# Low halves of the weights in two GpSimd operations each, and ScalarE's high halves placed ahead of its waits in one projection

## The reference, cut to what matters

```python
def second_block(x, ...):
    h = rmsnorm(x, ln1_g[l])
    proj = h @ w_in[l]
    b_a, c_a, x_a, x_b, g_b, gate_a_logit, gate_b_logit = jnp.split(proj, SPLIT_POINTS, axis=-1)
    y_a = b_a * causal_depthwise_conv(c_a * x_a, conv_a_w[l])
    u_b = causal_depthwise_conv(x_b, conv_b_w[l], conv_b_b[l])
    y_b = rg_lru(u_b, lru_wa[l], lru_ba[l], lru_wx[l], lru_bx[l], lru_lambda[l])
    y_b = y_b * jax.nn.gelu(g_b)
    ...
```

## Time and profile before

| | us |
|---|---|
| median of 3 runs (lowest, highest) | 1902.72 (1899.79, 1903.24) |
| the profiled execution's own time | 1900.95 |
| its span in the trace | 1898.9 |
| TensorE busy | 1763.8 |
| VectorE busy | 971.0 |
| GpSimd busy | 751.6 |
| ScalarE busy | 633.9 |

### The profile page before, as it was taken

One profiled execution on the slowest core, in us unless ns is written; L12 is line 12 of the kernel. 1 busy time (PEld: TensorE's weight loads), 2 busy tenths in 40 slices (PEclk: granted clock), 3 DMA queues, 4 the chain that ended last, 5 costly groups with the idle time before them and its releaser, 6 DMA issues.

```text
span 1898.9 us, 21690 instructions
## 1 busy us (share of the span) xinstructions
PE 1763.8 (93%) x7718; PEld 1424.0 (75%) x7718; DVE 971.0 (51%) x1285; ACT 633.9 (33%) x789; POOL 751.6 (40%) x312
## 2 busy tenths in 40 slices
PE   6899998885799898999999999999999999999996
PEld 4677875663678686888888877777888888888885
DVE  5752387888862447242334676767323343133136
ACT  3322342232242341122114456566333343222222
POOL 3342441113334143444444345455444444444442
PEclk9899998987899998999999999999999999999998
DMA  4232221111222022222222323232222222222222
GB/s 160 89 111 78 89 86 37 34 45 45 89 89 89 23 92 75 100 90 98 99 97 91 103 97 111 99 100 99 90 99 99 96 93 99 97 91 100 100 91 97
DMA packets 47695, 169.28 MB, mean 89 GB/s; under 512 B 5205, under 2 KB 5205, under 8 KB 47321
## 3 DMA queue, kind: packets, MB, share of 16 engines
q1 hardware_dynamic: 44640, 160.45, 24.6%
q10 hardware_dynamic: 3000, 8.09, 1.2%
HBM read 166.43 MB, written 2.10 MB: 89 GB/s over the span
## 4 chain that ended last, share of the span: by engine, by line
PE 29%; issue 29%; POOL 14%; DVE 1%; POOLq 0%; ACT 0%; DVEq 0%
POOL m_w_lo L439 14%; PE ps L471 10%; PE ps L473 10%; PE ps L472 10%; DVE m_h L1948 0%; DVE m_s L1209 0%; POOLq L447 0%; POOLq L445 0%; POOL m_QL L459 0%; DVE m_qs L1581 0%; PE ps L499 0%; DVE m_qs L1583 0%; DVE m_ftmp L1573 0%; DVE m_ftmp L1571 0%; DVE m_s L1923 0%
## 5 line engine op out<-in xcount | busy, mean ns | idle before, releaser
L439 POOL TENSOR_TENSOR m_w_lo<-m_raw,m_w_hi 128x1024 fp32r<-128x1024 f32 x302 | 737.2, 2444 | 1073.0 <-ACT m_w_hi L881 1072.8
L881 ACT ACTIVATE m_w_hi<-m_raw 128x1024 fp32r<-128x1024 f32 x302 | 318.1, 1056 | 652.6 <-DMA m_raw<-in_strips 648.9
L471 PE MATMUL ps<-m_XH,m_w_hi 128*128 128x512 f32 x1160 | 470.7, 406 | 10.6 <-POOL m_w_lo L439 8.8
L472 PE MATMUL ps<-m_XL,m_w_hi 128*128 128x512 f32 x1160 | 455.6, 393 | 0.0
L473 PE MATMUL ps<-m_XH,m_w_lo 128*128 128x512 f32 x1160 | 455.4, 393 | 0.0
L471 PEld LDWEIGHTS ps<-m_XH,m_w_hi 128*128 128x128 f32 x1160 | 220.4, 190 | 75.9 <-POOL m_w_lo L439 17.5
L472 PEld LDWEIGHTS ps<-m_XL,m_w_hi 128*128 128x128 f32 x1160 | 220.6, 190 | 46.6 <-issue 2.4
L473 PEld LDWEIGHTS ps<-m_XH,m_w_lo 128*128 128x128 f32 x1160 | 220.1, 190 | 47.2
L471 PE MATMUL ps<-m_FH,m_w_hi 128*128 128x512 f32 x432 | 169.1, 391 | 2.9 <-DVE m_FL L1202 2.8
L472 PE MATMUL ps<-m_FL,m_w_hi 128*128 128x512 f32 x432 | 168.7, 390 | 0.0
L473 PE MATMUL ps<-m_FH,m_w_lo 128*128 128x512 f32 x432 | 168.6, 390 | 0.0
(11 more groups left out here) (310 smaller groups left out, 2260.1 us busy)
## 6 DMA issues: line engine op xcount, KB each, us to landing
m_raw<-in_strips SPq DMA_DIRECT2D x302, 512.0 KB, 3.2
m_x_in<-in_x ACTq DMA_DIRECT2D x8, 256.0 KB, 4.3
m_x_res<-in_x ACTq DMA_DIRECT2D x1, 2048.0 KB, 8.0
out<-m_h SPq DMA_DIRECT2D x8, 256.0 KB, 2.1
m_memf<-in_mem ACTq DMA_DIRECT2D x1, 1024.0 KB, 10.2
m_decay<-in_decay ACTq DMA_DIRECT2D x1, 1024.0 KB, 14.9
m_w<-in_w ACTq DMA_DIRECT2D x1, 512.0 KB, 13.3
m_skip<-in_skip ACTq DMA_DIRECT2D x1, 512.0 KB, 3.7
```

Source lines behind the costliest of these rows:

```text
L439: nc.gpsimd.tensor_tensor(w_lo[:, c], raw[:, c], f(w_hi[:, c]), ALU.subtract).then_inc(lo_ready, 1)
L471: pe.matmul(dst, w_hi[:, c], xh, start=first, stop=False)
L472: pe.matmul(dst, w_hi[:, c], xl, start=False, stop=False)
L881: act.activation(w_hi[:, c], raw[:, c], ACT.Copy).then_inc(hi_ready, 1)
```

## The change

`low` writes a strip's low half in two operations of 512 columns, each of which counts `lo_ready` up by one, so every wait for it on TensorE is doubled; TensorE still waits for both. In `lru_turn` three of the six `ahead` calls of a turn move up in ScalarE's list: w4's ahead of the wait for `m_pX`, w5's ahead of the wait for the convolution, and w3' into the turn before, between the square and the square root. In the first turn w3's stays where it was; the last turn gives none for the strips after it, which the next loop does.

```diff
@@ GpSimd @@
             def low(slot):
-                c = slice(slot * STRIP, (slot + 1) * STRIP)
-                nc.gpsimd.tensor_tensor(w_lo[:, c], raw[:, c], f(w_hi[:, c]), ALU.subtract).then_inc(lo_ready, 1)
+                for part in range(2):
+                    c = slice(slot * STRIP + part * (STRIP // 2), slot * STRIP + (part + 1) * (STRIP // 2))
+                    nc.gpsimd.tensor_tensor(w_lo[:, c], raw[:, c], f(w_hi[:, c]), ALU.subtract).then_inc(lo_ready, 1)
@@ TensorE, and so at six more waits @@
-                pe.wait_ge(lo_ready, n + 1)
+                pe.wait_ge(lo_ready, (n + 1) * 2)
@@ ScalarE, lru_turn @@
                 n = S_IN + mt * 6
-                ahead(n)
                 if mt == 0:
+                    ahead(n)
                     root(4)
                     root(5, acc)
+                ahead(n + 1)
                 act.wait_ge(in_free[0], mt + 1)
                 act.activation(xtap[:], pX[:, 3:T + 3], ACT.Identity, bias=col("cbb", mt), scale=col("cb3", mt)
                                ).then_inc(x_tap, 1)
-                ahead(n + 1)
+                ahead(n + 2)
                 act.wait_ge(u_full, mt + 1)
                 act.activation(uH[:], t2[1][:], ACT.Copy).then_inc(u_high, 1)
-                ahead(n + 2)
                 act.wait_ge(a_in, mt + 1)
...
                 act.activation(a_sq[:], t2[8][:], ACT.Square).then_inc(lru_e, 1)
+                if mt < KT - 1:
+                    ahead(n + 6)
                 act.wait_ge(lru_q, mt + 1)
```

More of the change, by code:

```diff
@@ L722, in _ @@
             for u in range(4):
-                pe.wait_ge(lo_ready, S_WOUT + u + 1)
+                pe.wait_ge(lo_ready, (S_WOUT + u + 1) * 2)
                 for k in range(4, KT):
@@ L832, in in_turn @@
                     n = v * 6 + 5
-                    pe.wait_ge(lo_ready, i * 12 + (S_IN + n + 1))
+                    pe.wait_ge(lo_ready, (i * 12 + (S_IN + n + 1)) * 2)
                     pe.wait_ge(u_pair, mt + 1)
```

## The result

The changed kernel takes 1873.3 us (median of four runs, 1868.13 to 1876.67) beside 1902.49 for the kernel before, a ratio of 0.9847 [0.9822, 0.9871]. The forecast was 1886 with a range of 1876 to 1898: right in direction, too small by 13 us, and the range missed.

What follows compares the result with a forecast made beforehand. A closed ring of VectorE and ScalarE, stretched by GpSimd's low halves, was taken to bound the input projection. 1900.95 - 14 (projection) - 3 (elsewhere) = 1884, with the median 1.8 us above: 1886 us, range 1876 to 1898.

Steps and rivals of the forecast that it cites:

- Elsewhere: Outside the input projection, only the split acts, mainly in the first 520 us: 3 us gained, bounds 0 to 24.
- The projection: In the input projection's seven turns and the merge's head, split and moves together gain 14 us.
- the ring: VectorE and ScalarE handing work to each other in each projection turn: 31.09 us, falling to 29.15, TensorE alone 28.56.
- four late starts: In each projection turn, strips w3, w4, w0' and w1' start late on TensorE, losing 2.5 us over four.
- Rival 1: GpSimd holds VectorE over both halves, 2.5 us or more; projection turn near 31 us, total 1898 to 1904; chance 0.07.
- Rival 2: A half costs far more than half, from 1.6 us the projection loses; at 1.7 us total 1914; chance 0.04.
- Rival 3: Modest gain: halves of 1.35 to 1.45 us, projection gains 5 to 9, nothing outside; 1893 to 1898; chance 0.16.
- Rival 4: More gained outside the projection, 12 us, with TensorE the limit in the projection; about 1873; chance 0.13.
- 22 low halves: Low halves in early mLSTM, convolution, query and key stretches; each could give back up to about 1.1 us.

Runs made afterwards that it cites:

- e3: Kernel before, with two operations per strip everywhere except the input projection and the first four merge strips: 1887.09 us, 0.9911.
- e5: Kernel before, with two operations only for the 58 strips up to the long convolution's end: 1892.88 us, 0.9951.
- e13: Kernel before, with two operations only for the 12 z projection strips, whose low halves fall in the mLSTM stage: 1901.62 us, 0.9990.
- e8: Changed kernel, with two operations per strip only in the input projection and first four merge strips, whole elsewhere: 1886.53 us, 0.9914.
- e4: Changed kernel, with w3's high half moved behind the gelu, no longer ahead of the square root's table load: 1868.13 us, 0.9806.
- e11: The changed kernel itself, unaltered, measured again: 1868.05 us, 0.9824 of the kernel before.
- e2: Kernel before with only the moves in ScalarE's list, low halves whole: 1901.43 us, 0.9987.
- e1: Kernel before with only the split into two operations, ScalarE's list as before: 1868.52 us, 0.9806.
- e14: Kernel before, with each strip's low half in sixteen operations of 64 columns, ScalarE's list as before: 1917.28 us, 1.0073.
- e7: Kernel before, with each strip's low half in four operations of 256 columns, ScalarE's list as before: 1859.98 us, 0.9769.
- e10: Kernel before, with each strip's low half in eight operations of 128 columns, ScalarE's list as before: 1852.29 us, 0.9736.
- e12: Changed kernel, ScalarE's moves kept, with four operations of 256 columns per strip instead of two: 1855.84 us, 0.9755.
- e9: Kernel before, with GpSimd computing only 16 of 1024 low-half columns and filling the rest with a constant: 1815.67 us, 0.9541.

## Why the prediction was wrong, and where it was right

- **The step that failed is the term "Elsewhere".** I took 3 us, near the lower end of 0 to 24, "because most of VectorE's excess there is off TensorE's path". e3 measured 16.5: 10.3 in the first 58 strips (e5), some 6 behind them. The bounds held it; the choice between them had only two rows behind it and no sum over the held operations. The mechanism was the one written down, and its size was off by five times. It also acts where the term did not look: 3 to 5 us come at the start of the feed-forward part, behind the 520 us to which I had kept it, and part of those through TensorE's clock, for which the sum had no term. A sum over VectorE's groups would have shown more: 32 of the 128x128 products at 463 ns on average, one of which I had looked at. How it is divided between the first 58 strips is only partly shown: e13 found 4.5 us in its stage where I had expected 5 to 8, and 1.8 us in the time.
- **The projection** was forecast at 14 us and gave 16.6 (e8); the turn 28.87 us for 29.15, TensorE's waits 0.5 us for 8.8. The two sizes on the way were near: a half 1.29 us for 1.25, `m_pX`'s pair 2.46 us for 2.6, `m_BL` 1.66, no single operation above 2. GpSimd's added work was forecast at 30 us and is 69, hidden all the same.
- **The moves.** Of the 1.05 us that w3' ahead of the root was to cost the ring, 0.4 a turn is seen, some 2 to 3 us in all (e4 beside e11), with TensorE as the floor under the comparison; the rest is open. The earlier high halves, of which I made four late starts less, are worth 2 us alone (e2) and nothing measurable beside the split (e1, e4, e11): with the ring as short as TensorE's own work (e1), TensorE waits for no low half in the projection, early or not.
- **Rival 1**, that GpSimd holds over both halves, fell: VectorE's `m_yA` and the operation behind it end inside and right behind the pair at 1129.45. The rule of the Trainium skill beside it (GPSIMD Engine Reference, § 2.1 Instruction dispatch), read as the next Pool instruction starting at once, would have made it so; the pair's 3.40 us instead of 2.53 shows that here a waiting VectorE operation goes first. For shorter pieces the rival was not wrong: in e14 VectorE is held over more than 30 of them (10.09 us).
- **Rival 2** fell with the half's 1.29 us. The estimate by a straight line from the Trainium skill's GPSIMD Engine Reference, § 3.1 Elementwise — side-by-side cycle accounting, gave 1.35; the rows have a fixed part of 0.19 us, not 0.30.
- **Rival 3** fell: nothing of its slower halves was seen, and elsewhere gave more, not nothing.
- **Rival 4**, more elsewhere with TensorE the limit in the projection, is what happened, with its 1873. It had 0.13, and the range stopped at 1876, inside it. The range should have taken in the upper part of the bounds that I had written down myself. That its sum meets the first measurement so closely is luck: the second one is 1868.05, and 3 to 5 us came from a place outside its 22 low halves.
- **The expectations for single runs** missed mostly the same way. Below their ranges came e3, e4, e7, e10 and e12, by 2 to 3 us, and e9 by 29; e2, e5 and e8 missed by under 1 us; e14 came out 17 us above. Until the sixteenths I kept pricing the contention too low.

## What to carry to other kernels

Where two engines shut each other out of SBUF, as VectorE and GpSimd do here, the length of one operation is the length of the other's wait, as long as they take turns (here down to pieces of 0.741 us; at 0.464 with three exceptions, at 0.325 no longer): cut the long ones of the engine with time to spare, until its busy time, contention included, comes near the pace of the engine that sets the time (here 25.6 us a turn beside TensorE's 28.56 is the best tried, 34.1 is too much). Read that busy time off a trace; a product of piece count and undisturbed length leaves the contention out. Before pricing such a change, list the waiting engine's operations that are longer than their undisturbed length over the whole program, and take the sum on the waited-for path, not a handful of rows. An engine at 51% busy can be a good part waiting: here 184 of 971 us.

## What the hardware showed that I had not expected

- The busy time of VectorE fell by 184 us with no instruction of its own changed (e9), and the kernel by 87 us, though VectorE's busy share of the span was 51% at most.
- Between two GpSimd operations that are both ready, VectorE's waiting operation gets its turn with pieces of 1.29 and 0.741 us; this is what makes splitting work. With pieces of 0.464 us it fails three times in e10 (about 4 us each), with 0.325 us often, once for 10.09 us (e14).
- The fixed part of such a GpSimd operation is 0.19 us in its recorded length and 0.145 us in the spacing of neighbours, so that even eight pieces a strip pay.
- A held VectorE operation can cost TensorE twice: 2.8 us of waiting for `m_FL`, and a granted clock of 0.75 and 0.91 in the 10 us from 750 on, where e3 has neither.
